# The opening of a two-block network kernel: input transfers ahead of the first weight unit, its halves loaded apart, and low passes last in the first two units

## The reference, cut to what matters

```python
def rms_norm(x, g):
    xf = x.astype(jnp.float32)
    y = xf * lax.rsqrt(jnp.mean(xf * xf, axis=-1, keepdims=True) + EPS)
    return (y * g.astype(jnp.float32)).astype(x.dtype)

def short_conv_mixer(h, w_in, conv_k, w_out):
    b, c, u = jnp.split(h @ w_in, 3, axis=-1)
    y = lax.conv_general_dilated(c * u, conv_k[:, None, :], ...)   # causal, width 3, one filter a channel
    return (b * y) @ w_out

h = rms_norm(x, mix_norm[0])                    # x is [1, 512, 1024]
x = x + short_conv_mixer(h, conv_w_in[0], conv_kernel[0], conv_w_out[0])   # conv_w_in[0] is [1024, 3072]
```

## Time and profile before

| what | value |
|---|---|
| median of 3 runs | 2125.05 us (2122.46 to 2125.62) |
| the profiled execution | its span is 2120.0 us, from first to last instruction; its whole time is not listed apart from the three above |
| TensorE busy | 2063.2 us, 97% of the span |
| VectorE, ScalarE, GpSimdE busy | 44%, 37%, 51% |
| bytes moved | 177.83 MB, 84 GB/s over the span |
| granted TensorE clock | 0.993 of full speed, mean |

### The profile page before, as it was taken

One profiled execution on the slowest core, in us unless ns is written; L12 is line 12 of the kernel. 1 busy time (PEld: TensorE's weight loads), 2 busy tenths in 40 slices (PEclk: granted clock), 3 DMA queues, 4 the chain that ended last, 5 costly groups with the idle time before them and its releaser, 6 DMA issues.

```text
span 2120.0 us, 27333 instructions
## 1 busy us (share of the span) xinstructions
PE 2063.2 (97%) x10652; PEld 1708.1 (81%) x10652; DVE 936.7 (44%) x1430; ACT 782.1 (37%) x1126; POOL 1074.1 (51%) x899
## 2 busy tenths in 40 slices
PE   8999999999999999999999989999999999999998
PEld 6878888888787778888888768888887878888886
DVE  3184433322234343434222687888883214434321
ACT  4123222222244343222132454454463235553442
POOL 4454555545433234545555387888883432323342
PEclk9999999999999999999999999999999999999999
DMA  4223332233422213333233221222222331122131
GB/s 164 92 87 110 97 99 83 93 95 96 126 88 80 83 47 100 100 100 97 77 96 108 81 82 42 62 75 67 62 60 67 95 101 60 43 64 74 53 87 60
DMA packets 235402, 177.83 MB, mean 84 GB/s; under 512 B 9219, under 2 KB 231735, under 8 KB 235288
## 3 DMA queue, kind: packets, MB, share of 16 engines
q1 hardware_dynamic: 232716, 175.60, 27.4%
q10 hardware_dynamic: 2540, 0.56, 0.1%
q0 software_dynamic: 32, 0.07, 0.0%
HBM read 173.73 MB, written 2.47 MB: 83 GB/s over the span
## 4 chain that ended last, share of the span: by engine, by line
PE 55%; issue 23%; POOL 15%; DVE 4%; ACT 1%; POOLq 0%; ACTq 0%; DVEq 0%
PE bank L1878 16%; PE bank L1879 15%; PE bank L1880 15%; POOL wlo L619 15%; PE bank L2317 1%; PE bank L2458 1%; PE bank L2269 1%; PE bank L2283 1%; PE bank L2313 1%; PE bank L2474 1%; DVE xc L1533 1%; PE bank L2472 0%; PE bank L2432 0%; PE bank L2244 0%; DVE ybuf L1588 0%
## 5 line engine op out<-in xcount | busy, mean ns | idle before, releaser
L619 POOL TENSOR_TENSOR wlo<-raw,whi 128x512 fp32r<-128x512 f32 (+1 forms) x668 | 856.3, 1313 | 974.0 <-ACT whi L706 974.0
L1878 PE MATMUL bank<-hHi,whi 128*128 128x512 f32 x1408 | 556.6, 395 | 7.7 <-DVE xT L1332 1.7
L1879 PE MATMUL bank<-hLo,whi 128*128 128x512 f32 x1408 | 549.1, 390 | 0.0
L1880 PE MATMUL bank<-hHi,wlo 128*128 128x512 f32 x1408 | 549.1, 390 | 0.0
L706 ACT ACTIVATE whi<-raw 128x2048 fp32r<-128x2048 f32 (+1 forms) x168 | 303.8, 1808 | 480.2 <-PE bank L1880 476.5
L1878 PEld LDWEIGHTS bank<-hHi,whi 128*128 128x128 f32 x1408 | 264.6, 188 | 77.8 <-issue 19.3
L1880 PEld LDWEIGHTS bank<-hHi,wlo 128*128 128x128 f32 x1408 | 264.7, 188 | 56.2
L1879 PEld LDWEIGHTS bank<-hLo,whi 128*128 128x128 f32 x1408 | 264.8, 188 | 54.4 <-issue 1.2
L1878 PE MATMUL bank<-whi,hHi 128*128 128x256 f32 x896 | 263.2, 294 | 6.2 <-ACT gO L1198 3.7
L1880 PE MATMUL bank<-whi,hLo 128*128 128x256 f32 x896 | 254.2, 284 | 0.0
L1879 PE MATMUL bank<-wlo,hHi 128*128 128x256 f32 x896 | 254.1, 284 | 0.0
(11 more groups left out here) (349 smaller groups left out, 2939.2 us busy)
## 6 DMA issues: line engine op xcount, KB each, us to landing
raw<-in_ssd_w_in SPq DMA_DIRECT2D x48, 512.0 KB, 4.8
raw<-in_ffn_w_gate SPq DMA_DIRECT2D x44, 512.0 KB, 4.7
raw<-in_ffn_w_up SPq DMA_DIRECT2D x44, 512.0 KB, 4.7
raw<-in_gla_w_in SPq DMA_DIRECT2D x40, 512.0 KB, 4.7
raw<-in_conv_w_in SPq DMA_DIRECT2D x24, 512.0 KB, 4.4
raw<-in_ffn_w_down SPq DMA_DIRECT2D x32, 384.0 KB, 3.4
raw<-in_attn_w_qkv SPq DMA_DIRECT2D x24, 512.0 KB, 4.6
raw<-in_ffn_w_down SPq DMA_DIRECT2D x32, 320.0 KB, 3.8
```

The source lines that it names most:

```text
L619: ins = pool.tensor_tensor(wlo[s][:, part], raw[s][:, part], whi[s][:, part].bitcast(F32), ALU.subtract)
L1878: pe.matmul(dst, hi1, hi2, start=first, stop=False)
L1879: pe.matmul(dst, hi1, lo2, start=False, stop=False)
L1880: return pe.matmul(dst, lo1, hi2, start=False, stop=last)
```

## The change

SP issues the four x tiles ahead of unit 0. Unit 0 is loaded in two transfers by output channel (`half_unit`: all eight k tiles, 128 channels each, rows of 512 B) and not by k. The first half counts up a semaphore of its own, `half_in`; the second counts `raw_full0`, which an increment of 16 completes. The `START_AT_ONE` increments stand ahead of unit 1's load. ScalarE makes the high part of each half apart: the first after the three squares and ahead of the `hHi` copies, the second between `hHi` 1 and `hHi` 2. GpSimdE makes the low parts in the same halves (`first_low`). TensorE takes unit 0 and unit 1 by `late_low`: first all high-weight passes, k by k through both banks, then, behind the wait for `w_lo`, all low-weight passes. VectorE's program is as it was.

```diff
             vector(*VEC_ROWS[0])
-            load(0, 0, cols(W, DM))
             for t in range(NT):
                 sp.dma_start(m_in["xtok"][:, DM * t:DM * (t + 1)], A["x"][0, P * t:P * (t + 1), :]).then_inc(S(f"x_in{t}"), 16)
+            for b in range(2):
+                sp.dma_start(half_unit(raw[0], b), cols(W, DM + P * b, P)).then_inc(S("half_in") if b == 0 else raw_full[0], 16)
+            sp.sem_inc(raw_full[0], 16)
+            for name in START_AT_ONE:
+                sp.sem_inc(S(name), 1)
             load(1, 1, cols(W, 2 * DM))
...
+            def first_low():
+
+                for b in range(2):
+                    pool.wait_ge(S("half_hi") if b == 0 else w_hi, 1)
+                    for q in range(2):
+                        ks = slice(4 * q, 4 * q + 4)
+                        dst, src, hi = (half_unit(t, b)[:, ks, :] for t in (wlo[0], raw[0], whi[0]))
+                        ins = pool.tensor_tensor(dst, src, hi.bitcast(F32), ALU.subtract)
+                ins.then_inc(w_lo, 1)
...
-            high(0, 0)
             for t in range(NT - 1):
                 token_square(t)
+            act.wait_ge(S("half_in"), 16)
+            act.activation(half_unit(whi[0], 0), half_unit(raw[0], 0), ACT.Copy).then_inc(S("half_hi"), 1)
             act.wait_ge(S("vec_ready"), 1)
             for k in range(KT):
                 act.wait_ge(S("x_turn"), k + 1)
                 copy(tile(hHi, k), bank[k][:, :], S("h_hi"), scale=gain(0, k))
+                if k == 1:
+                    act.wait_ge(raw_full[0], 32)
+                    act.activation(half_unit(whi[0], 1), half_unit(raw[0], 1), ACT.Copy).then_inc(w_hi, 1)
...
+            def late_low(s):
+
+                pe.wait_ge(S("cu_done" if s else "c_ready"), 1)
+                for part in range(2):
+                    if part:
+                        unit(s)
+                    for k in range(KT):
+                        x = slice(SEQ * k, SEQ * (k + 1))
+                        if s == 0 and part == 0:
+                            pe.wait_ge(h_ready, k + 1)
+                        for b in range(2):
+                            dst, w = bank[2 * s + b][:, :], slice(256 * k + P * b, 256 * k + P * (b + 1))
+                            if part == 0:
+                                if k == 0:
+                                    pe.wait_ge(*((w_hi, s + 1) if s or b else (S("half_hi"), 1)))
+                                    pe.wait_ge(res_done, 2 * s + b + 1)
+                                pe.matmul(dst, whi[s][:, w], hHi[:, x], start=k == 0, stop=False)
+                                pe.matmul(dst, whi[s][:, w], hLo[:, x], start=False, stop=False)
+                            else:
+                                ins = pe.matmul(dst, wlo[s][:, w], hHi[:, x], start=False, stop=k == KT - 1)
+                                if k == KT - 1:
+                                    mark(ins)
...
-            gated(0)
+            late_low(0)
+            constants()
+            late_low(1)
             with pe.Fori(1, 4) as i:
                 gated(i)
```

More of the change, by code:

```diff
@@ L297, in bc, with half_unit @@
             return ap.unsqueeze(2).broadcast_to([ap.shape[0], ap.shape[1], n])
+        def half_unit(buf, b):
+            return v3(buf[:, :], KT)[:, :, P * b:P * (b + 1)]
         def rep(ap, n):
@@ L478, in _ @@
             sp.dma_start(m_in["vrows"][32:64, 2 * P:3 * P], A["ssd_conv_b_2"].rearrange("a (r p) -> (a r) p", p=P)).then_inc(S("vec_in"), 16)
-            for name in START_AT_ONE:
-                sp.sem_inc(S(name), 1)
             with sp.Fori(1, 4) as i:
@@ L675, in _ @@
             if on("ssd"):
-                for u0, u1 in ((0, U_DOWN0), (U_DOWN0, U_QKV), (U_QKV, U_DOWN1), (U_DOWN1, U_SSD), (U_SSD, U_SSD + 2)):
+                first_low()
+                unit_low(1)
+                for u0, u1 in ((2, U_DOWN0), (U_DOWN0, U_QKV), (U_QKV, U_DOWN1), (U_DOWN1, U_SSD), (U_SSD, U_SSD + 2)):
                     lows(u0, u1)
@@ L692, in _ @@
             else:
-                lows(0, u_end)
+                first_low()
+                unit_low(1)
+                lows(2, u_end)
         @block.scalar
@@ L1956, in gated @@
                     pe.wait_ge(S("cu_done" if s else "c_ready"), 2 * i + 1)
-                    first = isinstance(i, int) and s == 0
                     for b in range(2):
[L1959 to L1970, removed]
@@ L1972, in _ @@
-            gated(0)
+                        mark(chan(bank[2 * s + b][:, :], s, pair(b), hHi, hLo, range(KT)))
+            def late_low(s):
[19 more added lines that the diff above has]
+                                    mark(ins)
@@ new lines, in constants @@
+            def constants():
+                pe.wait_ge(res_done, KT)
+                other_vectors()
+                spread(0)
+                if on("attn"):
+                    pe.wait_ge(S("bias_in"), 32)
+                    pe.wait_ge(S("rb_one"), 1)
+                    pe.matmul(bank[5][0:HEADS, :], m_toe["rb"][:, :], m_toe["bkt"][:, 0:SEQ], start=True, stop=True).then_inc(S("toe_mm"), 1)
+                    pe.matmul(bank[6][0:HEADS, 0:P], m_toe["rb"][:, :], m_toe["bkt"][:, SEQ:640], start=True, stop=True).then_inc(S("toe_mm"), 1)
```

## The result

The changed kernel takes 2128.24 us (median of 13 runs, 2127.13 to 2130.70), the kernel before, run beside it on the same chips, 2122.46 us (13 runs, 2121.50 to 2125.77). The ratio is 1.0025, 95% interval [1.0018, 1.0033]: slower by 5.8 us by the medians, 3.8 to 7.0 by the interval. The forecast was +5.6 us (2130.6 on a median of 2125.05). The kernel before came out 2.6 lower here than in the three runs that the forecast was added to, so 2130.6 is 2.4 too high as a time, while the difference is right.

What follows compares the result with a forecast made beforehand. TensorE, busy 97% of the span, was taken as the bound, so only its holes or clock drops matter. A bank wait of +3.2 and low clock of +2.4 gave +5.6 on 2125.05, so 2130.6 us; range 2127.0 to 2133.5.

Steps and rivals of the forecast that it cites:

- T: Landing time of unit 0's first half in the opening, taken as 11.1 us, bounds 10.1 and 12.4.
- The hole: Unit 0: TensorE stands after two matmuls until VectorE's copy of xT 1; +3.2 us, bounds +2.2 and +4.5.
- Theory L: Rival in e1's forecast: unit 0's hole waits for ScalarE's high part of unit 1; stays to about 20, +5.8 us.
- The clock: TensorE restarts in unit 0 at the low clock for about 5.2 us; +2.4 us, 1.9 to 3.0.
- B: Rival: unit 0's stall comes but TensorE restarts at full clock; +3.2, 2128.3 us, chance 0.18.
- D: Rival: xT copies come in time, so bank 1 causes no hole in unit 0; -1.6, 2123.4 us, chance 0.05.
- C: Rival: unit 0's second half issued or landed late, holding ScalarE between hHi 1 and 2; costs 2.1, 2132.7 us, chance 0.13.
- the loss for rows of 512 B: Unit 0's half transfers, with 512 B rows, were taken to be some 0.2 us longer each.

Runs made afterwards that it cites:

- e1: Changed kernel with VectorE's copy of xT tile 1 moved from behind all eight low parts to right behind the second; 2124.03 us, ratio 1.0006.
- e2: The e1 kernel with the last transpose made 24 times more, filling the gap ahead of the first product; 2122.39 us, ratio 0.9996.
- e3: Changed kernel with the late_low loops turned, all k into bank 0, then all k into bank 1, VectorE untouched; 2123.36 us, ratio 1.0004.
- e7: Changed kernel, bank 1 wait kept, with 24 extra transposes and 22 extra products before the first real one; 2125.48 us, ratio 1.0016.
- e4: Kernel before with the regrouped passes of units 0 and 1 alone, transfers, ScalarE and GpSimdE as before; 2129.69 us, ratio 1.0032.
- e5: Kernel before with x transferred ahead of a whole unit 0 and ScalarE's high part of unit 0 behind the three squares; 2128.49 us, ratio 1.0030.
- e8: Kernel before with the regrouped passes and the copy of xT 1 right behind the second low part; 2123.12 us, ratio 1.0005.

## Why the prediction was right

Step by step, predicted against the changed kernel's trace:

| step | predicted | measured |
|---|---|---|
| first x tile landed, transposes start | 4.8 | 4.90 |
| first half landed (T) | 11.1 | 11.6; 10.7 to 10.9 in e1, e2, e3 and e7 |
| second half landed | 12.8 | 13.3; 12.4 to 12.6 in e1, e2, e3 and e7 |
| first product | T+3.3 = 14.4 | 14.76 |
| copy of xT 1 starts | T+7.8 = 18.9 | 19.33 |
| TensorE gets bank 1 | 19.85 | 20.15 |
| low clock after it | 5.2 us | 5.1 us (20.15 to 25.3) |
| last product of unit 0 | 30.05+2.4 | 32.85 |
| shift of unit 1 | +5.6 | +6.0 |
| shift far down | the same | +5.8 at 1259 us |

**The hole (+3.2).** The bare wait for the copy of xT 1 was read from VectorE's order in the earlier trace rows and the new loop, and e1, e3 and e4 show it from three sides: move the copy, turn the loop, or take the loop alone. From the restart at 20.15, 45 distances of 0.2265 would put the last product of unit 0 at 30.34, 3.5 later than before; the other 2.5 of the 6.0 are the clock. Theory L, which the view of waits suggests, failed in e1.

**The clock (+2.4).** Shown by e7 (2.5, with the wait for bank 1 kept and both empty stretches filled) and, for the first stretch beside a short hole, by e2 (1.6). The prediction took the two stretches together as nearly empty, which is how it came out: the fall is at 15.0, ahead of the hole. The reading that led to it was the transposes of the earlier trace rows. It was a little off: those that start up to 12.8 still take 421 ns and the first short one starts at 13.0, 4.5 us behind the first and not 4.1. The granted clock of 1.00 in the opening's windows said nothing of the kind, and it also says 1.00 at 5 to 8 us in the changed kernel, where the transposes take 421 ns in the median and 272 later on.

**Rivals.** B (the clock holds) and D (no hole) are excluded by the timeline. C (the halves late) did not come about: the second half landed 0.5 later than I took it in this profile, at about 13.3, but ScalarE wanted it at 13.70.

**What was off.** T by 0.5 in the profiled run and by -0.2 to -0.4 in the others. As the end moves with T, and the profile before has its own, it is partly luck that 5.6 and 5.8 lie so close. Two errors in T nearly cancel: the loss for rows of 512 B was larger than the 0.2 taken (in e3 the two halves landed 1.8 and 1.7 us behind the transfer before them, in e5 the same 512 KB with rows of 1 KB 1.5 each, the x tiles with rows of 4 KB 1.3 to 1.4), but the fourth x tile landed at 8.9 there and not at 9.7. By the prediction's own sum T is 11.0 without that loss, so the time would be 0.1 lower and not the 0.2 it gives. And that a profiled span may be 3 us off for a reason far from the change was no part of the working.

That the loss is from the order of the passes, with VectorE's order, and not from the transfers is shown. Why the later low stretches differ in length between runs of one kernel is not; it was not tried.

## What to carry to other kernels

Before loops are regrouped so that a second buffer is wanted sooner, look at who frees it, in that engine's own order: here one small copy stood behind eight other jobs, free of cost only because 24 matmuls on the first buffer covered it. An empty stretch on TensorE costs more than its length when the clock is low behind it: 2.5 us more in the changed kernel (3.9 and 4.4 us empty, two products between them), about 1.5 in e4 (1.3 and 4.5). And where an instruction waits for two semaphores, check the profile's label against the counts in the code.

## What the runs showed of the hardware that I had not expected

- The first transposes run at the low level (421 ns) although the windows give 1.00 up to the first recorded fall: in an opening the durations tell the clock, not that column. When they speed up differs between runs, 2.8 us behind the first of them in e8, 4.5 before, 5.8 in e4: all 32 took 5.94 us in the profile of before, 5.14 in e8, 6.59 in e4, with the same program up to there.
- Work that computes nothing keeps the clock up: 24 repeated transposes (2.8 us) held it at 1.00 where it was 0.57 in e1.
- The same transfers, in the same order, landed up to 0.94 us apart between profiles (first half taken at 10.66 in e7, at 11.60 in the changed kernel).
